# Moving the modulation sums, folding beta at another place and regrouping eight small matmuls in a delta-rule transformer kernel

## The reference, cut to what matters

```python
c_act = silu(c)
mod = c_act @ w_ada + b_ada            # six vectors of 1024: sh1, sc1, g1, sh2, sc2, g2
shf, scf = split(c_act @ w_ada_f + b_ada_f)   # two more, used only by the last norm of the first block
# per head (8 heads of 128), tokens in chunks; beta, g: one number per token and head
k_beta, v_beta = k * beta[..., None], v * beta[..., None]
lower = where(strict, k_beta @ k.T * decay, 0)
t_inv = inverse(eye + lower)
u, w = t_inv @ v_beta, t_inv @ (k_beta * exp(g)[..., None])
v_new = u - w @ state                  # chunk by chunk, then o and the new state
```

## Time and profile before

| | |
|---|---|
| median of three runs | 2160.65 us (2157.55 to 2160.72) |
| the profiled execution | 2158.29 us |
| its span, first to last instruction | 2156.5 us |
| TensorE busy | 2110.0 us, 98% |
| VectorE, ScalarE, GpSimd busy | 1322.8, 854.6, 399.0 us |
| bytes moved by DMA | 217.34 MB, 101 GB/s |
| granted TensorE clock, mean | 0.994 |

### The profile page before, as it was taken

The page is one execution under the profiler, slowest core; times in us unless marked ns, Lnnn a source line. Parts: engine busy times, 40 slices in busy tenths (PEclk is TensorE's granted clock), DMA queues, the critical chain, the costliest instruction groups (busy, mean ns, idle before and its releaser), DMA issues.

```text
span 2156.5 us, 29548 instructions
## 1 busy us (share of the span) xinstructions
PE 2110.0 (98%) x10250; PEld 1725.3 (80%) x10250; DVE 1322.8 (61%) x1919; ACT 854.6 (40%) x1353; POOL 399.0 (19%) x315
## 2 busy tenths in 40 slices
PE   6999999999999899999999999999999999999999
PEld 4788888888888788888888888888777777888887
DVE  6877788777554544443567555634788867555422
ACT  3333333333232233332335444422566635545322
POOL 0555676555600400000110000011000000000000
PEclk9999999999999999999999999999999999999999
DMA  8344433344333323333332333333221123333322
GB/s 298 109 118 117 126 108 107 107 117 117 109 97 117 108 84 95 95 96 92 96 107 78 98 97 94 88 99 99 59 59 50 54 83 88 97 96 95 101 98 78
DMA packets 378032, 217.34 MB, mean 101 GB/s; under 512 B 7864, under 2 KB 368754, under 8 KB 376435
## 3 DMA queue, kind: packets, MB, share of 16 engines
q1 hardware_dynamic: 377155, 214.03, 33.5%
q0 software_dynamic: 288, 2.10, 0.3%
q10 hardware_dynamic: 528, 0.40, 0.1%
HBM read 212.31 MB, written 4.19 MB: 100 GB/s over the span
## 4 chain that ended last, share of the span: by engine, by line
PE 84%; DVE 10%; ACT 3%; issue 2%; DMA 1%; SPq 1%; DVEq 0%; POOL 0%; POOLq 0%; ACTq 0%
PE ps L2272 23%; PE ps L2274 23%; PE ps L2273 23%; PE ps L2448 4%; PE ps L2617 2%; PE ps L2615 2%; PE ps L2616 2%; DVE w_lo L1341 1%; PE ps L2299 1%; DVE small L2161 1%; DMA ada<-w_ada 1%; DVE gd_v_s L1497 1%; DVE a_sb L2194 1%; ACT at_swap L1233 1%; DVE a_t_lo L2170 1%
## 5 line engine op out<-in xcount | busy, mean ns | idle before, releaser
L2272 PE MATMUL ps<-h_hi,w_hi 128*128 128x512 f32 x1896 | 769.5, 406 | 7.7 <-DVE h_lo L1405 5.5
L2274 PE MATMUL ps<-h_hi,w_lo 128*128 128x512 f32 x1896 | 743.2, 392 | 0.0
L2273 PE MATMUL ps<-h_lo,w_hi 128*128 128x512 f32 x1896 | 741.2, 391 | 0.0
L1341 DVE TENSOR_TENSOR w_lo<-raw,w_hi 128x1024 fp32r<-128x1024 f32 x332 | 428.5, 1291 | 368.8 <-ACT w_hi L836 368.3
L836 ACT ACTIVATE w_hi<-raw 128x1024 fp32r<-128x1024 f32 x334 | 353.5, 1059 | 640.3 <-PE ps L2274 494.7
L2272 PEld LDWEIGHTS ps<-h_hi,w_hi 128*128 128x128 f32 x1896 | 358.1, 189 | 83.1 <-issue 16.9
L2274 PEld LDWEIGHTS ps<-h_hi,w_lo 128*128 128x128 f32 x1896 | 357.2, 188 | 78.0
L2273 PEld LDWEIGHTS ps<-h_lo,w_hi 128*128 128x128 f32 x1896 | 358.6, 189 | 64.9
L2272 PE MATMUL ps<-act_hi,w_hi 128*128 128x512 f32 x352 | 136.9, 389 | 0.0
L2273 PE MATMUL ps<-act_lo,w_hi 128*128 128x512 f32 x352 | 136.9, 389 | 0.0
L2274 PE MATMUL ps<-act_hi,w_lo 128*128 128x512 f32 x352 | 136.9, 389 | 0.0
(11 more groups left out here) (395 smaller groups left out, 2759.0 us busy)
## 6 DMA issues: line engine op xcount, KB each, us to landing
raw<-ffn_w_up SPq DMA_DIRECT2D x88, 512.0 KB, 3.7
raw<-w_in SPq DMA_DIRECT2D x72, 512.0 KB, 3.7
raw<-w_ffn_in SPq DMA_DIRECT2D x44, 512.0 KB, 3.7
raw<-ffn_w_down SPq DMA_DIRECT2D x38, 512.0 KB, 3.6
ada_w<-w_ada SPq DMA_DIRECT2D x32, 512.0 KB, 3.8
raw<-diff_w_qkv SPq DMA_DIRECT2D x24, 512.0 KB, 3.7
ada<-w_ada SPq DMA_DIRECT2D x8, 1024.0 KB, 12.4
ada_w<-w_ada_f SPq DMA_DIRECT2D x16, 512.0 KB, 3.7
```

The source lines that it names most:

```text
L1341: nc.vector.tensor_tensor(w_lo[:, tile.slot], raw[:, tile.raw], w_hi[:, tile.slot].bitcast(F32), SUB)\
L2272: nc.tensor.matmul(dst, w_hi[:, tile.slot, k], hi, start=first, stop=False)
L2273: nc.tensor.matmul(dst, w_hi[:, tile.slot, k], lo, start=False, stop=False)
L2274: return nc.tensor.matmul(dst, w_lo[:, tile.slot, k], hi, start=False, stop=last)
```

## The change

- Beta moves to the *column's* token. kb_rows (four transposes and its place in the order) goes. The scalar of the four instructions that form low is now S_KK = -beta/norm * 1/norm; L1644 and L1645 go. v is scaled by its norm's half (S_VB) instead of beta, k_beg by exp(g) alone; v_new is multiplied by S_KB and -1 as it leaves PSUM, w by -1. One more fill stands ahead of q_tokens, so a head keeps 32.
- Levels 4 and 5: two matmuls of two chunks each with 128 stationary columns, in place of four. Their results lie in more blocks, so the y copies of level 4 are four instead of two, of level 5 two instead of one, the u transposes of level 4 four instead of two, ScalarE's x and u two instead of one each. GpSimd copies the half of lower for level 5 into one piece (low_half, 128x256).
- Modulation in the heads: only w_ada's columns, as four tiles of two row blocks by 512 columns. ScalarE multiplies by c_act (`weighed`, two of 128x512 a tile, the scale a column) after levels 2 and 3, after w, and after the second o_squares. GpSimd adds (one, then two of 128x512 a tile, seven in all), after low_half. SyncE's order follows.
- w_ada_f's part goes into the first eight steps of the first feed-forward: 16 tiles, each multiplied and added by GpSimd, a transpose and a reduction on VectorE a step, one matmul ahead of the down products, and the tiny instructions after it.

```diff
-HEAD_FILL.update(y0=2, v_new0=2, o_turn=4)
+HEAD_FILL.update(q_tokens=2, y0=2, v_new0=2, o_turn=4)
@@ SyncE
             with sp.Fori(0, H - 2) as i:
                 head_tile(6, i)
+                head_tile(7, i)
                 ada_load(i, 2, i, 0)
-                ada_load(i, 3, i, 1)
-                head_tile(7, i)
-                ada_load(i, 4, i, 2)
                 head_tile(0, i + 1)
-                ada_load(i, 5, i, 3)
-                ada_load(i + 1, 0, i, 4)
+                ada_load(i, 3, i, 1)
                 head_tile(1, i + 1)
-                ada_load(i + 1, 1, i, 5)
-                for t in (2, 3, 4, 5):
+                ada_load(i + 1, 0, i, 2)
+                head_tile(2, i + 1)
+                ada_load(i + 1, 1, i, 3)
+                for t in (3, 4, 5):
                     head_tile(t, i + 1)
...
+                if f == 0:
+                    with sp.Fori(0, LATE_STEPS) as i:
+                        for j in range(2):
+                            up_tiles(j, i)
+                            sp.wait_ge(late_own, 8 * i + 4 * j + 4)
+                            sp.dma_start(late_w[:], w_ada_f[:, :, bass.ds(i * (2 * P) + j * P, P)]).then_inc(late_in, 16)
@@ GpSimd, a head
-                    if n in (1, 3):
-                        modulation(n // 2)
...
-                for j in (2, 3, 4, 5):
+                pool.wait_ge(g_pe, step(PE_STEPS, f"y{WHOLE_LEVELS - 1}", h))
+                nc.gpsimd.tensor_tensor(low_h..., chunks(gd["low"][:])[:, :, 64:P], ones..., MULT).then_inc(g_pool, 1)
+                for j in range(4):
                     modulation(j)
@@ ScalarE, a head
+                def weighed(j):
+                    act.wait_ge(ada_land[j % 2], 32 * h + 16 * (j // 2 + 1))
+                    for e in range(2):
+                        w = two_blocks(ada_w[:, j % 2])[:, e]
+                        k = 2 * j + e
+                        ada_k = nc.scalar.activation(w, w, ACT.Copy, scale=cact[:, 1, k:k + 1])
+                    ada_k.then_inc(ada_act, 1)
...
+                    if n in WEIGHED:          # (2, 3), at the end of the level
+                        weighed(WEIGHED.index(n))
                 after_pe("w")
-                nc.scalar.activation(gd["x_t"][:], bank(7), ACT.Copy).then_inc(g_act, 1)
+                nc.scalar.activation(gd["x_t"][:], bank(7), ACT.Copy, scale=-1.0).then_inc(g_act, 1)
                 if more:
                     ahead(4)
                 else:
                     second_gate(2)
                     second_gate(3)
+                weighed(2)
...
+                    if n == 1:
+                        weighed(3)
@@ VectorE, a head
+                nc.vector.scalar_tensor_tensor(col4(S_VB), col4(S_KSS), 0.5, col4(S_KN), MULT, MULT).then_inc(g_dve, 1)
+                own("kb")
+                nc.vector.tensor_tensor(col4(S_KK), col4(S_KB), col4(S_KN), MULT).then_inc(g_dve, 1)
...
-                after_pe("kb_rows")
-                own("pair_decay")
-                nc.vector.tensor_tensor(gd["u_t"][:], gd["u_t"][:], bank(7), MULT).then_inc(g_dve, 1)
-                nc.vector.tensor_tensor(gd["low"][:], gd["low_d"][:], bank(7), MULT).then_inc(g_dve, 1)
...
-                        for pair in range(2):
-                            y = nc.vector.tensor_copy(gd["y_t"][quadrant(2 * pair + 1), 0:P]..., y_half[quadrant(pair), :, quadrant(pair)])
+                        for j in range(2):
+                            for pair in range(2):
+                                y = nc.vector.tensor_copy(two_by_two(gd["y_t"][quadrant(2 * pair + 1), 0:P])[:, :, j],
+                                                          y_two[quadrant(2 * j + pair), :, j, quadrant(pair)])
...
-                    nc.vector.tensor_copy(part(gd["y_t"], n), part(bank(2), n)).then_inc(g_dve, 1)
+                    nc.vector.tensor_scalar(part(gd["y_t"], n), part(bank(2), n), small[:, S_KB + n:S_KB + n + 1], -1.0, MULT, MULT)\
+                      .then_inc(g_dve, 1)
@@ TensorE, a head
-                    for n in range(NC):
-                        ins = nc.tensor.matmul(y_half[:, n], low_s[:, 64 * n:64 * n + 64], halves(x_t[:], 0)[:, n], start=True, stop=True)
+                    for a in range(2):
+                        ins = nc.tensor.matmul(y_two[:, a], low_s[:, P * a:P * a + P], halves(x_t[:], 0)[:, 2 * a:2 * a + 2], start=True, stop=True)
...
-                fill("kb_rows")
-                after_dve("kb")
-                rows_of(7, S_KB).then_inc(g_pe, 1)
                 fill("q_tokens")
-                after_dve("kk_decay")
+                after_dve("lower")
```

More of the change, by code:

```diff
@@ L74 @@
 S_EG, S_ELAST, S_ELEFT, S_LEFT, S_OMS, S_ON = 28, 32, 36, 40, 44, 48
-S_KB, S_KBEG, S_KDEC, S_G = 52, 56, 60, 64
+S_KB, S_KK, S_VB, S_G = 52, 56, 60, 64
 S_POOL, S_SHSQ, S_SQX = 68, 72, 73
@@ L165, in stage @@
         return s
-PE_STEPS = ["kv_tokens", "g_rows", "kk_qk", "kb_rows", "q_tokens"]
-DVE_STEPS = ["kss", "decay_arg", "g_left", "kb", "q_g", "kk_decay", "pair_decay", "u_pairs", "lower",
+PE_STEPS = ["kv_tokens", "g_rows", "kk_qk", "q_tokens"]
+DVE_STEPS = ["kss", "decay_arg", "g_left", "kb", "vb_scale", "kk_scale", "q_g", "lower", "u_pairs",
              "u_diag", "x_pairs", "qk"]
 ACT_STEPS = ["k_squares", "exp_decay", "exp_g", "exp_g_rows", "exp_last", "exp_left", "q_squares"]
-POOL_STEPS = ["k_norm"] + [f"mask{_n}" for _n in range(WHOLE_LEVELS)] + ["low_pairs", "ada", "o_norm"]
+POOL_STEPS = ["k_norm"] + [f"mask{_n}" for _n in range(WHOLE_LEVELS)] + ["low_pairs", "low_half", "ada", "o_norm"]
 for _n in range(LEVELS):
@@ L371, in block_kernel @@
         act_lo = sb("act_lo", [P, KF, T], F32R, at=wide + 2048 * KF)
+        late_w = sb("late_w", [P, KD, P], at=wide + 4096 * KF)
+        late_x = sb("late_x", [P, 2 * P], at=wide + 4096 * KF + 4096)
+        late_s = masks[:, 0:2]
         bands = sb("bands", [P, NC, len(WINDOWS), BAND], at=wide)
@@ L1576, in short_in @@
                     if more:
-                        dve.wait_ge(g_pool, step(POOL_STEPS, "low_pairs", h))
+                        dve.wait_ge(g_pool, step(POOL_STEPS, "low_half", h))
                         dve.wait_ge(g_pe, step(PE_STEPS, f"y{LEVELS - 1}", h))
@@ L1933, in feed_forward @@
                           .then_inc(f_lo, 1)
+                if f == 0:
+                    with dve.Fori(0, LATE_STEPS) as i:
+                        up_pair(i)
+                        late_sums(i)
+                with dve.Fori(LATE_STEPS if f == 0 else 0, UPS) as i:
+                    up_pair(i)
+                if f == 0:
+                    late_vectors()
                 def down():
@@ L2503, in head @@
                         pe.wait_ge(g_pool, step(POOL_STEPS, "low_pairs", h))
+                    else:
+                        pe.wait_ge(g_pool, step(POOL_STEPS, "low_half", h))
                     if n:
@@ L2597, in down @@
                         last.then_inc(tile_done, 1)
+                if f == 0:
+                    pe.wait_ge(late_sum, LATE_STEPS)
+                    nc.tensor.matmul(ps[0:32, 4, 0:8 * LATE_STEPS], quad[:], late_part[:].rearrange("p i b -> p (i b)"),
+                                     start=True, stop=True).then_inc(late_pe, 1)
                 if f < 2:
```

228 lines of the change are left out of this document (134 added, 94 removed).

## The result

The changed kernel takes 2168.91 us (median of 6 runs, 2167.66 to 2170.67), the kernel before 2160.31 us in the same comparison: ratio 1.0044, 95% interval 1.0034 to 1.0054. It is **slower by 8.6 us**. The forecast was 2155.1, the range ended at 2164: wrong in sign, and outside the range.

A forecast was written before the change was run, and what follows sets the result against it. TensorE's issue was taken to bound the heads, with VectorE just as late in levels 4 and 5. Loop heads -5.6, last head -0.7, matmul +0.3, norm +0.5 make -5.5 us: median 2155.1 us, range 2147 to 2164.

The forecast's parts named there:

- VectorE's chain in levels 4 and 5: Level 4's y copies to the end of v's taps, loop heads: ends at 179.55 against 179.77, -0.2 us a head.
- rival 1: Level 4: GpSimd's second add goes ahead of the silu of k; +0.1 us a head, 2161.4 us; chance 0.28.
- Rival 5: Levels 4 and 5: small VectorE instructions at upper bounds, both GpSimd adds ahead; +1.1 us a head, 2168.4 us; chance 0.13.
- TensorE's slots: Heads: removing kb_rows gives -0.45 us; four wide groups in levels 4 and 5 give -1.45 where nothing else is late.
- rival 4: Levels 4 and 5: wide records cost double; only the last head feels it, +1.45 us, 2156.6 us; chance 0.04.
- Rival 3: Heads: TensorE's savings come back in full, VectorE's half copies nearly free; sum -15.8 us, 2144.9 us; chance 0.07.
- ScalarE: Level 4: two weighed multiplications (1.22 us) come first, so x is done at 175.4 where before it was 174.1.
- Rival 2: Level 4: ScalarE isn't late, x at 174.5; -1.6 us a head, 2149.5 us; chance 0.12.
- The first head: S_KK may hit GpSimd's next weight split, ending 1.2 us later or earlier; taken as 0 beyond a loop head's -0.8.
- The last head: Double fills cover the chain, -0.45 - 1.45 us; weighed(2) ahead of the late o_squares adds 1.2; sum -0.7 us.
- The late modulation: First feed-forward: GpSimd's 20 us fits the 21.8 us step, covered by four tiles; the added matmul costs +0.3 us.
- the norm: GpSimd's 2.1 us multiplication starts there and may hold VectorE's first blocks: +0.5 us, bounds 0 and +3.

The follow-up runs named there:

- the narrow version: Changed kernel with levels 4 and 5 back in four matmuls of 64 stationary columns, all else as changed: 2159.98 us, ratio 0.9997 to the kernel before.
- the version with all four moves: Changed kernel, second weighing behind x of level 4, lower ahead of q_g, two late-sum buffers, last head's third weighing ahead of other gates' work: 2155.47 us.
- the repaired version: The version with all four moves, plus levels 4 and 5 narrow and weight tile 9 ahead of the modulation's fourth load in the last head: 2151.55 us.

## Why the prediction was wrong

**VectorE's chain in levels 4 and 5**, -0.2 us, is the step that failed. By its own terms, from the start of the y copies:

| term | forecast | measured |
|---|---|---|
| y copies | 0.84 | 0.92 |
| w_lo | 1.25 | 1.22 |
| transposes start | 3.06 | 3.01 |
| transposes | 0.85 | 1.02 |
| silu of k | 0.70 | 1.72 |
| y copies of level 5 | 0.56 | 0.59 |
| taps of v | 2.05 | 2.53 |
| end | 7.21 | 8.97 |

The head came out 1.02 + 0.80 = 1.82 us above its forecast, the chain 1.76: this stretch is all of it. Three terms carry it. The silu (+1.02) is rival 1's lock, seen and priced, but given 0.28. My own clock times spoke for it: they put GpSimd's second add at 176.15 and the silu at 176.25, so the add was first, and the sum took 0.70 us for the silu all the same. The order came out as those times had it: from the start of the y copies the add begins at 3.95 us (3.81 forecast) and the silu asks at 4.06 (3.91 forecast). The silu then ends at 5.78 us, where rival 1 had 5.56, since an add takes 1.28 us and not the 1.04 I took from a GpSimd instruction elsewhere. The taps (+0.48) were a plain error. I put their length down to GpSimd because it was active, without a row of the same instruction beside an idle GpSimd. They read PSUM and take 2.53 us either way. The remaining 0.26 are the small instructions. Rival 1 had the mechanism, at +0.1 a head. Rival 5 had the size, 2168.4 us, in part by luck: it had the small instructions at +0.7 where they cost 0.26, both adds ahead of VectorE where only the second was, and nothing for the taps or for the 2.0 us of the first head (below).

**TensorE's slots** were right in size: kb_rows is gone, and a group of four wide records costs 0.45 us where nothing holds it, the narrow form 0.80 to 0.82 (level 4's inverse 0.87 to 0.89). So rival 4 fell. Rival 3 fell with the waits. But it is not the number of records that pays. The weight loads of a narrow group before and of a wide one after, each with the load of the large matmul behind it:
```profile
175.15 0.54 PEld L2466 LDWEIGHTS ps<-gd_x_t,gd_low 128*64 128x64 f32 x8 [0.36 <-issue]
175.76 0.19 PEld L2272 LDWEIGHTS ps<-h_hi,w_hi 128*128 128x128 f32 x1
```
```profile
174.71 0.64 PEld L2547 LDWEIGHTS ps<-gd_x_t,gd_low_d 128*128 128x128 f32 x4
175.28 0.19 PEld L2361 LDWEIGHTS ps<-h_hi,w_hi 128*128 128x128 f32 x1
```
Inside a group narrow records start 0.058 us apart and wide ones 0.11, also in level 4's inverse, which streams only half as many columns (32 and 64). So eight narrow ones take 0.46 us and four wide ones 0.45. The Trainium skill (TensorE: Matmul & The Clock Gate, LDWEIGHTS) has a load take time in proportion to its columns, and this spacing agrees. What the regrouping saves, some 0.36 us a group, lies at the group's edges. The first narrow load waits for nothing that the profile shows ("issue"), yet begins only with its own matmul, at 175.15, which is 0.33 us behind the start of the large one ahead; the first wide one begins at 174.71, during the large matmul, and its group starts 0.23 us behind that one. The next large matmul starts 0.15 us behind the last narrow record, but 0.03 us behind the last wide one. Why a narrow group is not loaded ahead is open.

**ScalarE** is late as forecast, x of level 4 done 2.98 us after the y copies began (3.06 forecast). Rival 2 fell.

**The first head** was taken as -0.8 with S_KK's bounds of 1.2 us either way; it was +3.0. I followed the tiny scales to the next split, but not q_g and lower behind them in VectorE's order. Of the 3.0, 1.0 is levels 4 and 5 less kb_rows, as in a loop head. The rest, 2.0, is this place, and the head lay 2.55 us lower with lower first.

**The last head.** The o2 group cost 1.13 us and costs 2.35: +1.2, as forecast. But TensorE waits 0.75 us for the y copies of level 4 there too, so the head is -0.1 and not -0.7: its double fills were not the full cover I took them for.

**The late modulation** was not hidden in full. Its own matmul costs 0.43 us (0.3 forecast), the norm 0.2 (0.5). But I summed each engine's work per step and missed the ring across steps: GpSimd on VectorE's last transpose, SyncE's queue on GpSimd, 1.5 us in this profile.

## What to carry to other kernels

When the clock times of a forecast put another engine's instruction first, let the sum go by them: here they did, and the sum did not. Ahead of a claim that an instruction is slowed by another engine, look for the same instruction where that engine is idle. When an instruction moves in an in-order queue, write down what follows it up to the next one that TensorE waits for, in the first and the last pass of the loop as well as in the middle: two tiny instructions cost 2 us here, and a weighing moved later freed 1.8 us in each loop head and cost 3 in the last. And a gain in TensorE's records is worth only what the chain beside it lets through: price one level at a time, for here level 5's regrouping paid and level 4's did not.

## What the runs showed of the hardware

- **A VectorE instruction is held by a GpSimd one when it reads two tensors in SBUF, and not when one is in PSUM.** Held: the silu of k (0.64 to 0.69 alone, 1.72), q_g (0.68, 2.87), the four-column kb (2.24). Not held: the taps (2.53, 2.54), lower (1.13), the copies and transposes from PSUM. The Trainium skill (SBUF — State Buffer, SBUF: two separate sides) says so of instructions with two SBUF inputs, and these rows agree. The hold lasts to the end of GpSimd's instruction, so between two GpSimd instructions a waiting VectorE instruction gets in: the silu of the narrow version does (1.01 us), and then the second add waits (two adds 2.97 us in place of 2.64).
- **Behind two long waits the clock fell.** Windows of the changed kernel's first head, of the last head of the version with all four moves, and of the repaired version's first head:
```profile
81.00:86.00 5.00, 1.58 (x7) 0.96 (x6) 5.00 (x8) 1.33 (x5) 3.44 (x2) 1.00 0.44 112
86.50:91.50 5.00, 5.00 (x20) 4.06 (x19) 4.53 (x8) 1.92 (x10) 2.96 (x2) 0.66 0.28 82
```
```profile
577.60:583.00 5.40, 5.33 (x21) 4.52 (x22) 0.91 (x2) 3.06 (x5) 2.56 (x2) 0.68 0.36 97
```
```profile
82.00:87.00 5.00, 3.90 (x19) 2.97 (x19) 4.86 (x9) 1.88 (x6) 4.19 (x2) 1.00 0.46 129
```
The clock is full while TensorE waits (3.66 us in the first, 2.06 us in the second, where it is 1.00 over 575.5 to 577.6) and falls when it works again, to 1.2 GHz for a part of the stretch. In the third TensorE waited 1.10 us, and it did not fall. So a long wait costs more than its own time.
- **Small VectorE instructions have a floor.** Four copies of 32 x 64 take 0.92 us, two of 32 x 128 0.58; four transposes of half the width 1.02, two whole ones 0.63. Halving the width saves 0.06 us of 0.29 in a copy.
